# The second layer's modulation row blocks computed as per-partition products on VectorE instead of matmuls on TensorE

## The reference

```python
sh1, sc1, gt1, sh2, sc2, gt2 = _modulation(c, mod_w[i], mod_b[i])      # silu(c) @ w + b, 6 vectors of 1024
csh1, ...                    = _modulation(c_ctx[None, :], mod_w[i], mod_b[i])
def _conv_ffn(h, w_in, conv_w, conv_b, w_out, grid):
    u, g = jnp.split(h @ w_in, 2, axis=-1)          # w_in 1024 x 5632, D_FF = 2816
    g = _dwconv_grid(g, conv_w, conv_b, grid)
    return (jax.nn.silu(g) * u) @ w_out
```

## Time and profile before

| | |
|---|---|
| median of 3 runs | 2542.48 us (2542.19 to 2542.75) |
| the profiled execution's own time | 2542.31 us |
| its span in the profile | 2540.5 us |
| TensorE busy (PE) | 2433.6 us, 96% |
| VectorE busy (DVE) | 1496.7 us, 59% |
| ScalarE busy (ACT) | 714.1 us, 28% |
| GpSimd busy (POOL) | 622.1 us, 24% |

### The profile page before, as it was taken

One profiled execution on the slowest core, in us unless ns is written; L12 is line 12 of the kernel. 1 busy time (PEld: TensorE's weight loads), 2 busy tenths in 40 slices (PEclk: granted clock), 3 DMA queues, 4 the chain that ended last, 5 costly groups with the idle time before them and its releaser, 6 DMA issues.

```text
span 2540.5 us, 35022 instructions
## 1 busy us (share of the span) xinstructions
PE 2433.6 (96%) x14154; PEld 1962.0 (77%) x14154; DVE 1496.7 (59%) x1612; ACT 714.1 (28%) x979; POOL 622.1 (24%) x207
## 2 busy tenths in 40 slices
PE   7989999999999989999999989798999999999997
PEld 5557777777777768998899978676677777777775
DVE  4466666666666664553533317714677666666776
ACT  3642211112111125553442233323211111111112
POOL 0012211122111234662221125500321222211222
PEclk9999999999999999999999989899999999999998
DMA  8552211222112243652121258323111111111103
GB/s 343 214 208 99 83 63 61 83 83 83 67 57 83 99 166 134 216 175 100 61 80 59 69 154 221 113 85 123 65 43 50 50 50 50 38 45 50 48 18 133
DMA packets 106250, 255.03 MB, mean 100 GB/s; under 512 B 8880, under 2 KB 62768, under 8 KB 91312
## 3 DMA queue, kind: packets, MB, share of 16 engines
q1 hardware_dynamic: 88592, 228.56, 26.1%
q10 hardware_dynamic: 17568, 25.17, 2.7%
HBM read 223.68 MB, written 30.02 MB: 100 GB/s over the span
## 4 chain that ended last, share of the span: by engine, by line
PE 88%; DVE 5%; DMA 2%; ACT 2%; issue 1%; SPq 0%; POOL 0%; ACTq 0%; DVEq 0%; POOLq 0%
PE ps L585 24%; PE ps L587 22%; PE ps L586 22%; PE ps L988 2%; PE ps L990 2%; PE ps L989 2%; PE ps L679 1%; DVE y_x L1961 1%; PE ps L1141 1%; PE ps L647 1%; PE ps L622 1%; PE ps L712 1%; PE ps L877 1%; PE ps L878 1%; PE ps L879 1%
## 5 line engine op out<-in xcount | busy, mean ns | idle before, releaser
L585 PE MATMUL ps<-hx_hi,w_hi 128*128 128x512 f32 x1552 | 615.3, 396 | 10.3 <-DVE hx_lo L2092 4.4
L586 PE MATMUL ps<-hx_lo,w_hi 128*128 128x512 f32 x1552 | 607.3, 391 | 0.0
L587 PE MATMUL ps<-hx_hi,w_lo 128*128 128x512 f32 x1552 | 607.1, 391 | 0.0
L1945 DVE SCALAR_TENSOR_TENSOR acc<-ps,fcv,acc 128x945 f32<-128x945 f32 (+2 forms) x352 | 430.1, 1222 | 266.0 <-ACT acc L1434 223.1
L2438 POOL TENSOR_TENSOR w_lo<-raw,w_hi 128x2048 fp32r<-128x2048 f32 x79 | 368.3, 4663 | 783.6 <-ACT w_hi L1386 355.9
L1961 DVE TENSOR_TENSOR y_x<-y_x,ps 128x1024 f32<-128x1024 f32 x336 | 409.9, 1220 | 117.7 <-PE ps L587 110.1
L585 PEld LDWEIGHTS ps<-hx_hi,w_hi 128*128 128x128 f32 x1552 | 293.0, 189 | 79.6 <-DVE hx_lo L2092 9.3
L587 PEld LDWEIGHTS ps<-hx_hi,w_lo 128*128 128x128 f32 x1552 | 293.1, 189 | 61.9
L586 PEld LDWEIGHTS ps<-hx_lo,w_hi 128*128 128x128 f32 x1552 | 293.4, 189 | 58.0
L2449 POOL TENSOR_TENSOR a_lo<-prod,a_hi 128x1024 fp32r<-128x1024 f32 x44 | 105.6, 2400 | 828.9 <-ACT a_hi L1452 828.9
L585 PE MATMUL ps<-a_hi,w_hi 128*128 128x512 f32 x704 | 292.1, 415 | 13.2 <-DVE y_x L1961 11.6
(11 more groups left out here) (295 smaller groups left out, 3350.9 us busy)
## 6 DMA issues: line engine op xcount, KB each, us to landing
raw<-in_ffn_w SPq DMA_DIRECT2D x66, 1024.0 KB, 5.2
raw<-in_ffn_w SPq DMA_DIRECT2D x66, 512.0 KB, 4.1
modw<-in_modw SPq DMA_DIRECT2D x48, 512.0 KB, 6.9
modw<-in_modw SPq DMA_DIRECT2D x24, 1024.0 KB, 4.9
raw<-in_mlstm_w SPq DMA_DIRECT2D x14, 1024.0 KB, 5.4
vch<-v_scr SPq DMA_DIRECT2D x18, 512.0 KB, 4.2
x_scr<-y_x ACTq DMA_DIRECT2D x32, 256.0 KB, 2.2
dmat<-row_scr SPq DMA_DIRECT2D x16, 512.0 KB, 5.7
```

The costliest lines, as they stand in the source:

```text
L585: pe.matmul(out, whi, hhi, start=first, stop=False)
L586: pe.matmul(out, whi, hlo, start=False, stop=False)
L587: return pe.matmul(out, wlo, hhi, start=False, stop=last)
L1945: dve.scalar_tensor_tensor(out, src, cv[:, t:t + 1], out, ALU.mult, ALU.add).then_inc(sem("tap_done"), 1)
```

## The change

From its second round on, a round is computed on VectorE. `mod_round(c, acc_)` multiplies each of the eight 128 x 256 tiles of the round by the condition's value of each partition, for both conditions, and accumulates in SBUF: 16 operations of 128 x 256, 2 of them plain products and 14 `scalar_tensor_tensor`. Each waits for the operation before the previous one. It stands behind `gate(c)` in VectorE's stream, in blocks 1 to 21 of the first pass, and behind `gate(19)` and `gate(20)` in the second pass. TensorE adds up the partitions: `mod_columns` is now four matmuls of a 128 x 128 tile of the sums with one column of ones (8 instructions in the trace, as float32 matmuls are two). It stands in the next block between parts 0 and 1, where the rows stood, and waits for the sixteenth product. Round 0 keeps its matmuls; ScalarE scales its rows with `fold` into the new buffer `macc`, ahead of the first `acc`. SyncE's load of a round now waits for the round before to be summed. In the second pass the columns of rounds 22 and 23 are both taken in block 21.

```diff
             def load_mod(c):
-                sp.wait_ge(sem("modw1_used"), c)
+                sp.wait_ge(sem("mod_sum"), c * 16)
                 sp.dma_start(modw1[:], a["modw1"][c]).then_inc(sem("modw1_in"), 16)
...
-            def mod_columns(first):
+            def mod_columns(c):
+                pe.wait_ge(sem("mod_sum"), c * 16 + 16)
+                last = isinstance(c, int) and c == MODR - 1
                 for b in range(2):
-                    mm = pe.matmul(ps[:, 3, MODW + 2 * b:MODW + 2 * b + 2], modrow1[:, P * b:P * b + P], fold[:],
-                                   start=(first and b == 0), stop=(b == 1), skip_group_check=True)
+                    for x in range(2):
+                        at_ = MODW + 2 * b + x + (4 if last else 0)
+                        mm = pe.matmul(ps[:, 3, at_:at_ + 1], (macc_last if last else macc)[:, x, P * b:P * b + P], ones[:, 0:1],
+                                       start=(b == 0 and x == 0 and not last), stop=(b == 1 and x == 1), skip_group_check=True)
                 mm.then_inc(sem("modcol1_ready"), 1)
...
                             pe.wait_ge(sem("a_done"), j + p.n0)
                             if mod_round_of is not None:
-                                mod_rows(p, mod_round_of)
+                                mod_columns(mod_round_of)
+                                if p.index:
+                                    mod_columns(mod_round_of + 1)
...
             def first_of_ctx():
                 ctx_in(0)
-                pe.wait_ge(sem("mod1_done"), FT)
                 pe.wait_ge(sem("a_done"), FT)
-                mod_columns(True)
+                mod_columns(FT - 1)
...
+            def mod_in(c):
+                act.wait_ge(sem("modcol1_ready"), c + 2)
+                at_ = MODW + (4 if isinstance(c, int) and c == MODR - 1 else 0)
+                act.activation(modt[:].rearrange("p s (c b) -> p s c b", b=2)[:, :, c + MODR, :],
+                               ps[:, 3, at_:at_ + 4].rearrange("p (b x) -> p x b", x=2), ACT.Copy).then_inc(sem("mod1_done"), 1)
...
+                if with_mod:
+                    act.wait_ge(sem("modcol1_ready"), 1)
+                    for x in range(2):
+                        ins = act.activation(macc[:, x, :], ps[:, 3, 0:MODW], ACT.Copy, scale=fold[:, x:x + 1])
+                    ins.then_inc(sem("mod_sum"), 16)
...
                 if j == 0:
-                    act.wait_ge(sem("modw1_used"), FT)
+                    act.wait_ge(sem("mod_sum"), 16 * FT)
...
+            def mod_round(c, acc_):
+                dve.wait_ge(sem("modw1_in"), c * 16 + 16)
+                if acc_ is macc:
+                    dve.wait_ge(sem("modcol1_ready"), c + 1)
+                for k in range(KT):
+                    for x in range(2):
+                        n = 2 * k + x
+                        if k == 0:
+                            ins = dve.tensor_scalar(acc_[:, x, :], modw1[:, k, :], c_pad[:, k, x:x + 1], None, ALU.mult)
+                        else:
+                            dve.wait_ge(sem("mod_sum"), c * 16 + (n - 1))
+                            ins = dve.scalar_tensor_tensor(acc_[:, x, :], modw1[:, k, :], c_pad[:, k, x:x + 1], acc_[:, x, :], ALU.mult, ALU.add)
+                        ins.then_inc(sem("mod_sum"), 1)
...
                     gate(i * 2 + 1, 1)
+                    if p.index == 0:
+                        mod_round(i * 2 + 1, macc)
                     conv(i * 2 + 2, 0)
                     add(i * 2 + 1, 1)
                     gate(i * 2 + 2, 0)
+                    if p.index == 0:
+                        mod_round(i * 2 + 2, macc)
...
                 add(FT - 2, 0)
                 gate(FT - 1, 1)
+                mod_round(FT - 1, macc)
                 if between is not None:
                     between()
                 add(FT - 1, 1)
```

More of the change, by code:

```diff
@@ L1408, in hi_tile @@
                 hi_part(K, "out")
-            def mod_columns(c):
-                return act.activation(modt[:].rearrange("p s (c b) -> p s c b", b=2)[:, :, c + MODR, :],
-                                      ps[:, 3, MODW:MODW + 4].rearrange("p (b x) -> p x b", x=2), ACT.Copy)
-            def ffn(p, after_rows=None, after_silu=None):
-                def mod_rows(c):
-                    alone = isinstance(c, int) and c in (0, FT)
-                    if alone:
-                        act.wait_ge(sem("modw1_used"), c + 1)
-                    else:
-                        act.wait_ge(sem("modcol1_ready"), c)
-                    ins = act.activation(modrow1[:], ps[:, 3, 0:MODW], ACT.Copy)
-                    if not alone:
-                        ins = mod_columns(c - 1)
-                    ins.then_inc(sem("mod1_done"), 1)
+            def mod_in(c):
[3 more added lines that the diff above has]
+                               ps[:, 3, at_:at_ + 4].rearrange("p (b x) -> p x b", x=2), ACT.Copy).then_inc(sem("mod1_done"), 1)
+            def ffn(p, after_rows=None, after_silu=None):
                 def tile(j, par, last=False, mod_round_of=None):
@@ L1436, in tile @@
                     if mod_round_of is not None:
-                        mod_rows(mod_round_of)
+                        if p.index:
+                            act.wait_ge(sem("modcol1_ready"), MODR + 1)
+                        mod_in(mod_round_of)
+                        if p.index:
+                            mod_in(mod_round_of + 1)
                     first = isinstance(j, int) and j == 0
@@ L1456, in ffn @@
                 with_mod = p.index == 0
-                tile(0, 0, mod_round_of=0 if with_mod else FT)
+                if with_mod:
[3 more added lines that the diff above has]
+                    ins.then_inc(sem("mod_sum"), 16)
+                tile(0, 0)
                 with act.Fori(0, FT // 2 - 1) as i:
-                    tile(i * 2 + 1, 1, mod_round_of=i * 2 + 1 if with_mod else None)
-                    tile(i * 2 + 2, 0, mod_round_of=i * 2 + 2 if with_mod else None)
-                tile(FT - 1, 1, last=not with_mod, mod_round_of=FT - 1 if with_mod else FT + 1)
+                    tile(i * 2 + 1, 1, mod_round_of=i * 2 if with_mod else None)
+                    tile(i * 2 + 2, 0, mod_round_of=i * 2 + 1 if with_mod else None)
+                tile(FT - 1, 1, last=not with_mod, mod_round_of=FT - 2 if with_mod else FT)
             def ctx_tile(j):
@@ L1968, in ffn @@
                 dve.wait_ge(sem("y_zero"), p.index + 1)
-                with dve.Fori(0, FT // 2 - 1) as i:
+                with dve.Fori(0, FT // 2 - 1 - p.index) as i:
                     conv(i * 2 + 1, 1)
@@ L1975, in ffn @@
                     gate(i * 2 + 2, 0)
+                    if p.index == 0:
+                        mod_round(i * 2 + 2, macc)
+                if p.index == 1:
+                    conv(FT - 3, 1)
+                    add(FT - 4, 0)
+                    gate(FT - 3, 1)
+                    mod_round(FT, macc)
+                    conv(FT - 2, 0)
+                    add(FT - 3, 1)
+                    gate(FT - 2, 0)
+                    mod_round(FT + 1, macc_last)
                 conv(FT - 1, 1)
```

39 lines of the change are left out of this document (16 added, 23 removed).

## The result

The changed kernel takes 2526.39 us (median of 4 runs, 2526.02 to 2527.64) where the kernel before takes 2542.44 beside it: ratio 0.9938, 95% interval 0.992 to 0.9955. The profiled execution has a span of 2524.2 us. Four executions of the kernel before in these sets took 3408 to 7168 us; the ratios leave them out, while the medians given here count them.

A forecast was written before the change was run, and what follows sets the result against it. TensorE, holding 88% of the chain that ended last, was taken as the bound. Terms -11.0 (blocks 2 to 21), -0.6, +2.5, +0.2 and -0.4 sum to -9.3 us from 2542.31, forecast 2533, range 2527 to 2550.

The forecast's parts named there:

- sign of being wrong: Prediction wrong if the products' pitch is above 0.42, or TensorE waits for VectorE by 0.5 or more in each block.
- VectorE's round: Sixteen products behind the gate: 6.08 us at pitch 0.39, plus 2.29 for one product shut out by GpSimd.
- The room: 9.55 us from gate to TensorE's next round place; products just fit, TensorE waits 0.0 to 0.1, taken as 0.05.
- TensorE's side: Between parts 0 and 1, eight column instructions make the round 1.04 to 1.26 us instead of 1.79; gain taken 0.60.
- Block 1: First pass: the columns of round 0 wait for ScalarE alone, which is long done; 0.6 us less.
- End of the first pass: Round 21 delays the context's work: first addition 3.0 us later, part of it regained; 2.5 us more, from 0 to 6.
- Second pass: Blocks unchanged; block 0 gains nothing from removed row matmuls, and products in blocks 19 and 20 fit the same room.
- Block 21's +0.2: Second pass: 16 column instructions, 1.44 to 1.88 us and 0.32, stand where 1.79 stood; 0.2 us more.
- Moved loads, round 0's scaling: Loads issued one block later, and block 0's taps some 2 us later behind ScalarE's scaling, both covered: nothing.
- Last stage: End of the kernel: four instructions go, 0.4 us less.
- rival with 0.75 in each block: GpSimd kept out by the row of products: round 6.08, TensorE waits for nothing, 2527 us; chance 0.08.
- the middle rival: No change: 0.25 to 0.75 us wait per block, or additions and taps setting its length; 2538 to 2547, chance 0.17.

The follow-up runs named there:

- `pad_32`: The kernel before with 32 tiny one-column memsets on VectorE ahead of the second pass, nothing else: 2541.82 us, ratio 1.0003.
- `peel_only`: The kernel before with VectorE's second-pass loop ended two blocks earlier and blocks 19 and 20 written out, modulation left on TensorE: 2541.44 us, ratio 1.0006.
- the second set: Both kernels measured again without an edit: before 2540.68 us, changed 2530.26 us (7 runs, ratio 0.9961).
- `longer_05`: The changed kernel with one more VectorE product of 128 x 512 per round in blocks 1 to 20 of the first pass: 2536.1 us, ratio 0.9983.

## Why the prediction came out as it did

The direction and the place of the gain were right; the sum was too small. By the stretches the changed kernel is 14.9 us shorter in its traces, and the medians of three sets say 16.05, 10.6 and 11.6. The forecast was 9.3. Of the 5.6 between it and the stretches, 1.5 are in the blocks, 1.0 in block 1, 1.4 at the end of the first pass, 1.5 in the second pass and 0.2 at the end. Neither sign of being wrong that the prediction named came: the pitch is 0.39 and the wait 0.11.

- *VectorE's round: right.* 8.37 us forecast, 8.30 found; pitch 0.39, one product stretched to 2.6 by GpSimd, 6.08 forecast without GpSimd and 6.15 found.
- *The room: right.* TensorE reached the columns with the round just over. The forecast's wait of 0.05 is 0.11, by the two versions with a shorter round; a weight load that is no longer covered was not in the forecast. That it is an edge is shown by the longer rounds, which are felt in full.
- *TensorE's side: the mis-sized term.* I took 0.60 from 0.53 to 0.75. Without the wait a block is 0.73 shorter (704.75 to 690.1 over 20), near the upper end. My reason for the lower end, that column instructions in the same place took 0.47, was the wrong row to be near to: the eight new ones take 0.80 in all, and with 0.32 behind them the round costs 1.12 where I had 1.19. The rest, 0.09, is a term that I put at nothing: the first row matmul started 0.32 after the last matmul of part 0 (480.08, 480.40), and the first column matmul starts 0.23 after it (507.11, 507.34). With the wait it is 0.62 and not 0.55, so 12.5 instead of 11.0.
- *Block 1: the mechanism was missing.* 0.6 was forecast, 1.6 found. The round stands there behind a wait of 4.2 us and runs at half clock, and the half clock that follows was shorter in the changed kernel's traces; why it was, stays open. The trace of before has that wait too (4.3 us ahead of the row matmuls at 195.20), and I priced the round by a row at full clock.
- *End of the first pass: right in mechanism, too high.* First addition 2.44 later (3.0 forecast); 1.1 of it is left at the last one (2.5 forecast). TensorE's half clock now falls on the columns and on the two groups that nobody waits for. I had named that and taken only 0.5 off for it.
- *Second pass: the step failed.* "Unchanged" was forecast; it is 1.3 shorter. The steps of the loop's odd blocks lost 0.9, as they do when only the code ahead of VectorE's loop changes (`pad_32`), and two blocks written out, with constants for registers, lost 0.5 (`peel_only`). The prediction put both at nothing without a reason; a gap of 0.25 beside gaps of 0.14 in the trace of before was the only hint. Block 21's +0.2 was right.
- *Moved loads, round 0's scaling: right at nothing.* The conversions start after the loads, as worked out, and no step of a block shows them.
- *Last stage: right by luck.* -0.4 was forecast for four removed instructions and -0.6 found, but versions that keep them are 0.5 and 0.9 shorter there.
- *The range.* It took its lower end from the gain in each block alone. Its own rival with 0.75 in each block adds up to -15.6 and -0.5, which from 2542.5 is 2526.4 and not 2527. That this is the measured time is luck: that rival had GpSimd kept out by the row of products, and it was let in (one product of 2.6). The lower end of the middle rival has a like slip, -5 by its terms and not -4. And the median of a set can lie several us from that of another, 16.05 below against 10.6, which was not in the range; the second set's median of 2530.26 lies inside it.

The rule of the Trainium skill that spoke against the change ("VectorE: DVE Perf Modes", "The DRAIN you can't avoid") would have made the round 1.25 longer, as the prediction estimated it from its rows. The trace doesn't agree here either: fifteen starts lie 0.08 before the recorded end of the operation before, and fourteen of these operations wait for a semaphore. The section itself excepts an operation that is not held by the one before, which the prediction left out; whether these are such operations no run here shows.

## What to carry to other kernels

- Work that is moved to another engine's idle room is worth what the bounding engine saves, until its end meets the place of the wait. Find that place from both sides: a product more and a few less tell at once how much is in hand. Here it was nothing, and still 0.6 us per block were gained.
- In these traces a GpSimd operation cost VectorE nothing beside additions with an operand in PSUM (1.22 us each beside GpSimd's 4.54 and 4.61), and most of its length beside operations with both in SBUF: 2.15 of its 2.40 in a row of products, while four operations of 128 x 8 took 5.24 instead of 0.52, until GpSimd had ended. Reordering a few instructions for that gave 7.4 us, two thirds of the 11.6 that the change itself gave in that set.
- Read single terms from the steps of a repeated marker (here the gates, steady to 0.05), not from the time, which scattered by more than 10 us between executions of one kernel.

## What the runs showed of the hardware that was not expected

- A wait of 1.06 us and eight small matmuls behind it put TensorE at half clock in some blocks of one program and not in others; where it did, 1.6 us were lost on top. A wait of 0.25 to 0.27 in each of 19 blocks (`longer_05`) never did.
- The same loop of VectorE has a gap of 0.25 or 0.14 us between its first two taps in odd blocks: 32 tiny operations placed ahead of it, which shift its code, changed the one into the other, and the pass was 1.1 us shorter in that trace.
- A matmul whose weight load is held back shows no idle time in PE's row, yet the group took 0.92 instead of 0.80 us: the wait (0.29) stands in PEld's row, and 0.11 of it was felt.
- The time lay above the span by 1.8 us in all runs of the kernel before and by 1.8 to 3.1 in those of the changed one. The cause is open.
